# A 31-tap convolution moved from VectorE to 32-column matmuls on TensorE, and a decay's fall computed on ScalarE

## The chip, the core and the metric

The kernel runs on one core of a Trainium2 chip. A core has TensorE (PE: matmuls, results in PSUM; its weight loads are shown apart as PEld), VectorE (DVE), ScalarE (ACT), GpSimd (POOL) and SyncE (SP), each with its own instruction queue worked off in program order, and 16 DMA engines that they share. Engines wait for one another on semaphores. The metric is the device time of the whole program in microseconds.

## The reference

Two blocks follow each other on a sequence of 512 frames with 1024 features: a Mamba-2 layer, a windowed attention layer, then a layer with a convolution and pooling mixer and a feed-forward part, then a layer with an HGRN2 mixer and a feed-forward part. What the change touches:

```
# mamba2_mixer -> ssd_chunked: 32 heads in 8 groups, chunks of 128 frames
a_cs  = cumsum(dt * A) within a chunk                  # falls within the chunk
seg   = a_cs[..., :, None] - a_cs[..., None, :]
decay = exp(where(causal, seg, -inf))
y_diag = einsum((C B^T) * decay, x)
y_off  = einsum(C, h_in, exp(a_cs))

# conv_pool_mixer: z = h @ w_in  (512 value, 512 gate, 512 pool channels)
a = a_val * sigmoid(a_gate)
a = causal depthwise convolution of a, 31 taps, 512 channels, + dw_b
a = silu(layernorm(a, ln_g, ln_b))
for window w in (2, 4, 8, 16), 128 channels each:
    d = mean of the last w frames of u - u;   p = (d @ pool_w[g]) * pool_scale
return concat([a, p]) @ w_out
```

## The kernel before

Features lie on the 128 partitions and the 512 frames on the free axis, so a "tile" is 128 features by 512 frames. All projections are one stream of matmuls with weights from HBM. A float32 weight w is split in two (`wh`, and `wl` = the rest), and so is the activation (`hh`, `hl`); each product is three matmuls (L644 to L646, in the first units of a phase L613 to L615). A unit is 256 columns of a weight. It is loaded in two halves through a ring of four slots: SP loads a half into `stage` (L510), POOL writes `wh` and the negated `wl` (L566, L567) and issues a DMA that adds `stage` onto `wl` (L570). PE makes one tile with 8 x 3 matmuls per 128 columns and puts it in one of four PSUM banks `gp`; DVE takes it out, times `rstd`, and gives the bank back. Nothing plans the order at run time: each engine's program is written out, and generators interleave the projection's granules (half a tile each) with the mixer's own work (`run(gran, n)`).

**Mamba (`mamba`).** The loop goes over 8 groups g and one more round; in each round there are six slots. The projection's tiles of group g are made while the mixer works on group p = g - 1. In slot 0 PE transposes x and B and multiplies C B^T (`turn_and_cb`, L705 to L716); this waits for the SiLU (L1154) of the last of the four short convolutions (L1589, DVE). In slots 1 and 2 PE spreads `a_cs` of two heads each over the partitions (`spread`, L727, banks `mp0` and `mp1`). ACT makes `EC` = exp of it (L1170). DVE picks the chunk's last value (`cd`, L1619) and writes the fall within the chunk to `G`, four pieces of 128 columns a head (`segment`, L1623: min and subtract). ACT takes exp of `G` (L1174), and DVE multiplies (`products`, L1631 and L1633). In slot 2 DVE also carries the states (`recur`, L1637 to L1644). `y_tile` (L748, L752) is in slots 4 and 5: two heads side by side, each with 64 of the 128 output partitions.

**Convolution and pooling (`conv_pool`, called "cp" below).** The projection has 12 tiles: sigmoid gates 0 and 1, values 2 and 3, gates 4 and 5, values 6 and 7, pool channels 8 to 11. The gated values go to `apad` (c_a) with 30 zero columns in front. Channel tiles 0, 1 and 2 are convolved on DVE, one instruction per tap (L1928, L1932: 31 x 3), and the takes of projection tiles 4 to 11 are placed after every fourth tap. Channel tile 3 is convolved on PE (L877): 31 float32 matmuls of 128 x 128 diagonal matrices, which ACT builds before its sigmoids (L1277). POOL computes the window means (`window_means`, L529 to L549) in its queue behind the second unit of the output projection. After the four pool matmuls (L884) and the four matmuls that sum the channels (L891), a layernorm on DVE and ACT, and the output projection.

**Start.** The parameters come in 19 small DMAs, 9 on ACT's queue (behind one for the identity) and 10 on SP's, ahead of the first weights on SP's queue.

Of the kernel before, what the change touches and what calls it, by code (L numbers as in the profile page):

```python
# [34 lines left out]
P = 128  # L35
# [17 lines left out]
CW = 31  # L53
POOLW = (2, 4, 8, 16)
# [13 lines left out]
N_PAR = 19  # L68
# [121 lines left out]
def build(nc, x, positions, pre_norm, post_norm, ssm_w_in, ssm_conv_w, ssm_conv_b, ssm_dt_bias,  # L190
# [50 lines left out]
    with ExitStack() as ctx:  # L241
# [27 lines left out]
        class Region:  # L269
# [74 lines left out]
        apad = R.take("c_a", [P, 4, CW - 1 + L])  # L344
# [7 lines left out]
        taps = R.take("c_taps", [P, CW, P])  # L352
# [62 lines left out]
        taps_ready, gated_ready, last_conv, last_ready, pool_step = (sem(s) for s in (  # L415
            "taps_ready", "gated_ready", "last_conv", "last_ready", "pool_step"))
# [50 lines left out]
        def load_parameters(eng, half):  # L467
# [17 lines left out]
            else:  # L485
                rows(0, 0, P, ssm_conv_w.rearrange("o k (t p) -> (o k t) p", p=P))
                rows(1, 0, CW * 4, cp_dw_w.rearrange("o k (t p) -> (o k t) p", p=P))
# [41 lines left out]
        def window_means(pool):  # L529

            steps = 0
            for g in range(4):
                tile_taken(pool, tiles_of("cp")[0] + 8 + g)
                src, w = ub[:, g, :], 1
                while w < POOLW[g]:
                    dst = ws[:, 0 if w in (1, 4) else 1, :]
                    pool.tensor_tensor(dst[:, 2 * w - 1:], src[:, 2 * w - 1:], src[:, w - 1:16 + L - w],
                                       ALU.add).then_inc(pool_step, 1)
                    steps += 1
                    pool.wait_ge(pool_step, steps)  # L540
                    src, w = dst, 2 * w
                d = window_out(g)
                pool.tensor_scalar(d, src[:, 16:], 1.0 / w, 1.0, ALU.mult, ALU.mult).then_inc(pool_step, 1)
                pool.wait_ge(pool_step, steps + 1)
                pool.tensor_tensor(d[:, 0:16], src[:, 16:32], cst[:, C_RC + 16 * g:C_RC + 16 * g + 16],
                                   ALU.mult).then_inc(pool_step, 1)
                steps += 2
                pool.wait_ge(pool_step, steps)
                pool.tensor_tensor(d, d, ub[:, g, 16:], ALU.subtract).then_inc(window_ready, 1)  # L549

        @block.gpsimd
        def _(pool):
            count = [0] * HALVES
            for q, (u, i) in enumerate(halves):
# [22 lines left out]
                if u == phases["cp_out"][0] + 1:  # L577
                    window_means(pool)
# [3 lines left out]
        def _(pe):  # L582
# [90 lines left out]
            for k in range(KT):  # L673
                if k == 4:
                    pe.wait_ge(par_landed, 16 * N_PAR)
                    pe.wait_ge(skip_ready, 1)
                    for s, rows in enumerate((P, CW * 4, P, 48)):
                        mm = pe.transpose(mp[0][:, s * P:s * P + rows], prow[0:rows, s, :], ident[0:rows, 0:rows])
                    mm.then_inc(prm_turned, 1)
# [191 lines left out]
            def conv_pool():  # L871
                run(h_granules("cp", "pre2", LEAD["cp"], lambda: sum_squares(pre_round[2])))

                pe.wait_ge(gated_ready, 4)
                for i in range(CW):
                    pe.wait_ge(taps_ready, i + 1)
                    mm = pe.matmul(mp[1][:, :], taps[:, i, :], apad[:, 3, i:i + L], start=(i == 0), stop=(i == CW - 1))  # L877
                mm.then_inc(last_conv, 1)
                pe.wait_ge(poolw_landed, 16)
                for g in range(4):  # L880
                    pe.wait_ge(window_ready, g + 1)
                    if g >= 2:
                        pe.wait_ge(hi_ready, split0["cp"] + g - 1)
                    pe.matmul(mp[2 + g % 2][:, :], poolw[:, g, :], window_out(g), start=True,  # L884
                              stop=True).then_inc(pool_ready, 1)
                for t in range(4):
                    if t < 3:
                        pe.wait_ge(conv_ready, t + 1)
                    else:
                        pe.wait_ge(last_ready, 1)  # L890
# [150 lines left out]
        def _(act):  # L1041
# [82 lines left out]
            def mamba():  # L1124
# [46 lines left out]

                def decay_between(g, h):
                    act.wait_ge(seg_ready, 4 * g + h + 1)
                    act.activation(G[:, h, :], G[:, h, :], ACT.Exp).then_inc(dec_ready, 1)  # L1174
# [1025 lines left out]
```

## Time and profile before

| | us |
|---|---|
| median of 3 runs (2032.0 to 2037.17) | 2033.22 |
| the profiled execution, its own time | 2037.46 |
| its span, first to last instruction | 2035.7 |
| PE busy / weight loads | 1889.5 / 1497.6 |
| DVE busy | 1184.6 |
| POOL busy | 937.8 |
| ACT busy | 584.5 |

The span covers nearly all of the execution's own time (1.8 us lie around it). The profiled execution is 4.2 us (0.2%) above the median. PE is busy for 93% of the span, but a busy PE is not always a PE at full rate: the granted clock has a mean of 0.967. Of the slices of 50 us, most between 950 and 1600 us have PE busy from end to end; the mamba phase lies at about 60 to 440 us and the convolution's at about 785 to 950 us.

### The profile page before, as it was taken

The page shows a single profiled execution, that of the slowest core. Times are in us where ns is not written, and L with a number is a line of the kernel's source. Part 1 is how long each engine was busy: PE and PEld are TensorE (multiplying, and loading weights), DVE is VectorE, ACT ScalarE, POOL GpSimd, SP SyncE. Part 2 cuts the span into 40 slices and gives each one's busy share as a digit, 9 for nine tenths or more (in the row PEclk, how much of TensorE's full clock was granted, in tenths as well). Part 3 has the DMA queues.
Part 4 walks back from the last instruction along what each step waited for, and adds up shares of the span by engine and source line. Part 5 has one row for each costly group of instructions (what it writes and reads, how often), then busy time and mean ns, then how long its engine had stood idle before and what let it go on. Part 6 is the DMA issues. An engine that isn't in the chain of part 4 may idle for free.

```text
span 2035.7 us, 24615 instructions
## 1 busy us (share of the span) xinstructions
PE 1889.5 (93%) x9408; PEld 1497.6 (74%) x9408; DVE 1184.6 (58%) x1890; ACT 584.5 (29%) x980; POOL 937.8 (46%) x934
## 2 busy tenths in 40 slices
PE   6999999897899987968999999999999899999997
PEld 5777777686577665725888888887777678888886
DVE  5889898862877756896433231246777763323202
ACT  4333333421433325113201100024666531111001
POOL 4443434344533235552555555654443245555552
PEclk9999999898999998988999999999999899999999
DMA  8767666567445445812888888887555378888884
GB/s 206 163 135 154 134 148 134 124 135 176 109 104 104 94 95 120 194 42 60 199 196 188 197 191 191 196 201 168 125 125 114 88 157 191 196 190 195 184 188 112
DMA packets 207988, 306.31 MB, mean 150 GB/s; under 512 B 20836, under 2 KB 163200, under 8 KB 207872
## 3 DMA queue, kind: packets, MB, share of 16 engines
q0 software_dynamic: 42912, 149.44, 43.0%
q1 hardware_dynamic: 163472, 153.78, 24.0%
q8 instruction: 75, 1.23, 0.2%
q10 hardware_dynamic: 1488, 1.52, 0.2%
q14 instruction: 41, 0.34, 0.1%
HBM read 153.18 MB, written 2.10 MB: 76 GB/s over the span
## 4 chain that ended last, share of the span: by engine, by line
PE 52%; DVE 7%; ACT 2%; issue 1%; POOL 0%; ACTq 0%; DVEq 0%; POOLq 0%
PE gp L644 16%; PE gp L645 15%; PE gp L646 15%; DVE c_acc L1932 4%; PE mp L944 1%; PE gp L614 1%; PE gp L613 1%; PE gp L615 1%; ACT c_taps L1277 0%; PE mp L985 0%; PE mp L994 0%; POOL sqsum L524 0%; ACT L1079 0%; PE mp L987 0%; PE mp L963 0%
## 5 line engine op out<-in xcount | busy, mean ns | idle before, releaser
L566 POOL TENSOR_SCALAR wh<-stage 128x1024 fp32r<-128x1024 f32 (+2 forms) x298 | 352.5, 1183 | 931.6 <-PE gp L646 893.6
L644 PE MATMUL gp<-hh,wh 128*128 128x512 f32 x1544 | 621.2, 402 | 15.4 <-POOL wh L566 5.4
L645 PE MATMUL gp<-hh,wl 128*128 128x512 f32 x1544 | 604.2, 391 | 0.0
L646 PE MATMUL gp<-hl,wh 128*128 128x512 f32 x1480 | 579.4, 392 | 0.0
L644 PEld LDWEIGHTS gp<-hh,wh 128*128 128x128 f32 x1544 | 292.3, 189 | 83.4 <-issue 17.2
L567 POOL TENSOR_SCALAR wl<-stage 128x1024 fp32r<-128x1024 f32 (+2 forms) x298 | 352.5, 1183 | 0.0
L645 PEld LDWEIGHTS gp<-hh,wl 128*128 128x128 f32 x1544 | 292.3, 189 | 59.5 <-issue 1.2
L646 PEld LDWEIGHTS gp<-hl,wh 128*128 128x128 f32 x1480 | 279.4, 189 | 60.1
L570 POOL DMA_DIRECT2D wl<-stage x298 | 264.1, 886 | 94.7 <-POOL wl L567 85.8
L1979 DVE TENSOR_TENSOR val<-gp,rstd 128x512 f32<-128x512 f32 x44 | 30.4, 692 | 203.9 <-PE gp L646 203.9
L1883 DVE TENSOR_TENSOR xT<-gp,xT 128x512 f32<-128x512 f32 x32 | 22.1, 690 | 211.3 <-PE gp L646 211.3
L644 PE MATMUL gp<-f_h,wh 128*128 128x512 f32 x352 | 137.2, 390 | 0.0
L646 PE MATMUL gp<-f_l,wh 128*128 128x512 f32 x352 | 137.0, 389 | 0.0
L645 PE MATMUL gp<-f_h,wl 128*128 128x512 f32 x352 | 136.9, 389 | 0.0
L1056 ACT ACTIVATE f_h<-val 128x512 fp32r<-128x512 f32 x44 | 27.2, 633 | 277.1 <-DVE val L1985 277.1
L1975 DVE TENSOR_TENSOR sq<-gp,rstd 128x512 f32<-128x512 f32 x44 | 30.2, 691 | 114.2 <-PE gp L646 95.0
L1932 DVE SCALAR_TENSOR_TENSOR c_acc<-c_a,prm,c_acc 128x512 f32<-128x512 f32 x90 | 91.0, 1055 | 1.1
L1589 DVE SCALAR_TENSOR_TENSOR m_xs<-m_raw,prm,m_xs 128x512 f32<-128x512 f32 x96 | 84.3, 878 | 2.3
L646 PEld LDWEIGHTS gp<-f_l,wh 128*128 128x128 f32 x352 | 66.1, 188 | 13.7
L644 PEld LDWEIGHTS gp<-f_h,wh 128*128 128x128 f32 x352 | 66.1, 188 | 13.7
L645 PEld LDWEIGHTS gp<-f_h,wl 128*128 128x128 f32 x352 | 66.1, 188 | 13.6
L1985 DVE TENSOR_TENSOR val<-val,sq 128x512 f32<-128x512 f32 x44 | 72.7, 1692 | 0.0
(320 smaller groups left out, 2864.0 us busy)
## 6 DMA issues: line engine op xcount, KB each, us to landing
wl<-stage POOLq DMA_DIRECT2D x264, 512.0 KB, 5.4
stage<-ffn_w SPq DMA_DIRECT2D x120, 512.0 KB, 4.2
stage<-ssm_w_in SPq DMA_DIRECT2D x32, 512.0 KB, 5.1
stage<-hg_w_in SPq DMA_DIRECT2D x32, 512.0 KB, 4.3
stage<-ssm_w_in SPq DMA_DIRECT2D x32, 256.0 KB, 4.1
stage<-ssm_w_out SPq DMA_DIRECT2D x16, 512.0 KB, 4.8
stage<-att_w_in SPq DMA_DIRECT2D x16, 512.0 KB, 4.4
stage<-cp_w_in SPq DMA_DIRECT2D x12, 512.0 KB, 4.9
```

The lines of the kernel that those rows point to most:

```text
L566: pool.tensor_scalar(wh[:, s, part], stage[:, s, part], 1.0, 1.0, ALU.mult, ALU.mult).then_inc(hi_done, 1)
L567: pool.tensor_scalar(wl[:, s, part], stage[:, s, part], -1.0, 1.0, ALU.mult, ALU.mult).then_inc(neg_done, 1)
L570: pool.dma_start(wl[:, s, part], stage[:, s, part], accum_op=ALU.add).then_inc(lo_landed[s], 16)
L644: pe.matmul(bank[:, :], wvh[:, cols], hi(kk), start=start, stop=False)
L645: pe.matmul(bank[:, :], wvl[:, cols], hi(kk), start=False, stop=False)
L646: mm = pe.matmul(bank[:, :], wvh[:, cols], lo(kk), start=False, stop=stop)
L1056: act.activation(dst, val[:, n % 2, :], ACT.Copy).then_inc(hi_ready, 1)
L1589: ins = dve.scalar_tensor_tensor(v, raw[:, n % 2, i:i + L], prm[:, col:col + 1], v, ALU.mult, ALU.add)
L1932: ins = dve.scalar_tensor_tensor(acc[:, c, :], src, w, acc[:, c, :], ALU.mult, ALU.add)
L1975: dve.tensor_tensor(sq[:, j, :], gp[t % 4][:, :], rstd[:, :], ALU.mult).then_inc(bank_read[t % 4], 1)
L1979: dve.tensor_tensor(value_slot(n0 + 2 * n + j), gp[t % 4][:, :], rstd[:, :], ALU.mult).then_inc(bank_read[t % 4], 1)
L1985: dve.tensor_tensor(value, value, sq[:, j, :], ALU.mult).then_inc(value_ready, 1)
```

## The change

1. **Mamba's fall within a chunk goes to ACT.** `segment` on DVE becomes `chunk_decay`, which keeps the `cd` copy alone. ACT computes relu(f - value) from PSUM, four pieces a head, where f is the fall at the row's frame; its sign is turned back by `scale=-1.0` in the exp.

2. **The convolution goes to PE for all four channel tiles.** Four taps and 32 channels are put together on the 128 partitions: `shifted[t]` holds, for block b of 32 channels, four copies of it that are shifted by 0 to 3 frames. 16 DMAs a tile, of 32 partitions x 540 columns each, bring them from `apad`; ACT issues them. One matmul then does 4 taps of 32 channels (a 128 x 32 weight matrix, 512 frames) into 32 of the 128 PSUM partitions; 8 tap groups x 4 blocks are 32 matmuls a tile. DVE builds each tile's weights with one multiplication of 128 x 1024 (`tap_matrix`). ACT adds the bias from PSUM. The first two tiles are convolved between projection tiles, the others behind them.

3. **The window means go from POOL to DVE**, each behind the take of its tile.

4. The tap parameters come in 9 DMAs instead of one (27 parameter DMAs instead of 19), in pieces of 32 numbers, all on SP's queue. `shifted` lies where `ch` and `cl` are written later.

```
+                def fall_within(g, h):
+                    if h == 0 and g == 0:
+                        act.wait_ge(tok_ready, 1)
+                    for c in range(NCH):
+                        s = slice(c * P, (c + 1) * P)
+                        f = tokT[:, 0, c, HPG * g + h:HPG * g + h + 1]
+                        ins = act.activation(G[:, h, s], mp[h % 2][:, s], ACT.Relu, bias=f, scale=-1.0)
+                    ins.then_inc(seg_ready, 1)
...
                         if g > 0 and slot in (1, 2):
                             for h in pair:
                                 decay_to_start(p, h)
+                                fall_within(p, h)
...
-                    for c in range(NCH):
-                        s = slice(c * P, (c + 1) * P)
-                        f = tokT[:, 0, c, HPG * g + h:HPG * g + h + 1]
-                        ins = dve.tensor_scalar(G[:, h, s], mp[h % 2][:, s], f, f, ALU.min, ALU.subtract)
```

On PE:

```
+                def convolve(t):
+                    pe.wait_ge(taps_ready, t + 1)
+                    pe.wait_ge(shifts_landed[t], 16 * SHIFTS * SHIFTS)
+                    if t >= 2:
+                        pe.wait_ge(conv_ready, t - 1)
+                    for m in range(8):
+                        for b in range(SHIFTS):
+                            mm = pe.matmul(mp[t % 2][b * CB:(b + 1) * CB, :], taps[:, m, t, b, :],
+                                           shifted[t % 3][:, b, m * SHIFTS:m * SHIFTS + L],
+                                           start=(m == 0), stop=(m == 7))
+                    mm.then_inc(conv_whole, 1)
+
+                run(gran, 16)
+                convolve(0)
+                run(gran, 4)
+                convolve(1)
+                run(gran)
+                convolve(2)
                 pe.wait_ge(poolw_landed, 16)
                 for g in range(4):
                     pe.wait_ge(window_ready, g + 1)
...
+                convolve(3)
+                pe.wait_ge(conv_ready, 3)
```

On ACT, in place of the 31 diagonal matrices:

```
+                def shift(t):
+                    act.wait_ge(gated_ready, 2 * (t // 2 + 1))
+                    if t == 3:
+                        act.wait_ge(conv_whole, 1)
+                    for d in range(SHIFTS):
+                        for b in range(SHIFTS):
+                            act.dma_start(shifted[t % 3][d * CB:(d + 1) * CB, b, :],
+                                          apad[b * CB:(b + 1) * CB, t, d:d + GW]).then_inc(shifts_landed[t], 16)
...
                 for half in range(2):
                     for j in range(2):
                         t = t0 + 4 * half + j
                         tile_taken(act, t)
                         act.activation(sig[:, j, :], sig[:, j, :], ACT.Sigmoid).then_inc(sig_ready, 1)
+                    shift(2 * half)
+                    if half == 0:
+                        shift(1)
+                add_bias(0)
+                shift(3)
+                add_bias(1)
+                add_bias(2)
```

On DVE:

```
+                def tap_matrix(t):
+                    cols = prm[:, P_DW:P_DW + P].rearrange("p (m r) -> p m r", m=8)[:, :, SHIFTS * t:SHIFTS * (t + 1)]
+                    step(dve.tensor_tensor(taps[:, :, t, :, :],
+                                           eye[:, :].unsqueeze(1).unsqueeze(1).to_broadcast([P, 8, SHIFTS, CB]),
+                                           cols.unsqueeze(3).to_broadcast([P, 8, SHIFTS, CB]), ALU.mult))
...
                 for i in range(4):
                     take(i)
                 gate(0)
-                for n in convolve((0, 1)):
-                    if n % 4 == 2:
-                        take(4 + n // 4)
-                    if n == 15:
-                        gate(1)
-                for n in convolve((2,)):
-                    pass
+                for i in range(4, 8):
+                    take(i)
+                    tap_matrix(i - 4)
+                gate(1)
+                for g in range(4):
+                    take(8 + g)
+                    window(g)
+                dve.wait_ge(conv_whole, 4)
```

How the order of instructions moves. On ACT in slots 1 and 2 of mamba, before (m_EC is `EC`, m_G is `G`, m_tokT holds f):

```order
L1170 ACTIVATE m_EC<-mp 128x512 x2
L1147 ACTIVATE m_xs<-m_raw,prm 128x512
L1174 ACTIVATE m_G<-m_G 128x512 x2
L1170 ACTIVATE m_EC<-mp 128x512 x2
L1147 ACTIVATE m_xs<-m_raw,prm 128x512
L1174 ACTIVATE m_G<-m_G 128x512 x2
L1154 ACT_TABLE_LOAD
```

The same place on ACT in the changed kernel:

```order
L1170 ACTIVATE m_EC<-mp 128x512
L1178 ACTIVATE m_G<-mp,m_tokT 128x128 x4
L1170 ACTIVATE m_EC<-mp 128x512
L1178 ACTIVATE m_G<-mp,m_tokT 128x128 x4
L1147 ACTIVATE m_xs<-m_raw,prm 128x512
L1183 ACTIVATE m_G<-m_G 128x512 x2
L1170 ACTIVATE m_EC<-mp 128x512
L1178 ACTIVATE m_G<-mp,m_tokT 128x128 x4
L1170 ACTIVATE m_EC<-mp 128x512
L1178 ACTIVATE m_G<-mp,m_tokT 128x128 x4
L1147 ACTIVATE m_xs<-m_raw,prm 128x512
L1183 ACTIVATE m_G<-m_G 128x512 x2
```

Sixteen short activations a group are new in ACT's queue, ahead of the short convolution's last tap (m_xs<-m_raw) and of the exp of `G`; no table load is added. On DVE in slot 1, before:

```order
L1543 TENSOR_TENSOR m_raw<-gp,rstd 128x512
L1619 COPY m_cd<-m_EC 128x4
L1623 TENSOR_SCALAR m_G<-mp,m_tokT 128x128 x4
L1619 COPY m_cd<-m_EC 128x4
L1623 TENSOR_SCALAR m_G<-mp,m_tokT 128x128 x4
L1631 TENSOR_TENSOR m_G<-m_G,m_cbm 128x512
L1633 TENSOR_TENSOR m_EC<-m_EC,m_xs 128x512
```

The same place on DVE in the changed kernel:

```order
L1571 TENSOR_TENSOR m_raw<-gp,rstd 128x512
L1647 COPY m_cd<-m_EC 128x4 x2
L1652 TENSOR_TENSOR m_G<-m_G,m_cbm 128x512
L1654 TENSOR_TENSOR m_EC<-m_EC,m_xs 128x512
L1652 TENSOR_TENSOR m_G<-m_G,m_cbm 128x512
L1654 TENSOR_TENSOR m_EC<-m_EC,m_xs 128x512
```

Nothing stands any more between the copies and the products. On PE behind the last tile of the cp projection, before (c_pw the pool weights, c_dp and c_sig the window means):

```order
L646 MATMUL gp<-hl,wh 128x512
L877 MATMUL mp<-c_a,c_taps 128x512 x31
L884 MATMUL mp<-c_dp,c_pw 128x512 x2
L884 MATMUL mp<-c_sig,c_pw 128x512 x2
L891 MATMUL mp<-c_acc,ones 128x512 x4
```

The same place on PE in the changed kernel (c_s_ are the shifted copies):

```order
L633 MATMUL gp<-hl,wh 128x512
L868 MATMUL mp<-c_s_107,c_taps 32x512 x32
L884 MATMUL mp<-c_dp,c_pw 128x512 x2
L884 MATMUL mp<-c_sig,c_pw 128x512 x2
L868 MATMUL mp<-c_s_105,c_taps 32x512 x32
L891 MATMUL mp<-c_acc,ones 128x512 x4
```

Two of the four convolutions stand here; the other two stand ahead, with 48 projection matmuls (two tiles) between them and 48 behind the second.

## Rows read from the trace of the kernel before

**Rows 1.** Windows: start:end and length, busy (count) per engine, PE clock, DMA share, GB/s
```profile
134.17:168.36 34.19, 34.19 (x187) 26.95 (x186) 32.77 (x52) 11.04 (x17) 16.50 (x16) 1.00 0.73 150
178.02:223.54 45.52, 43.54 (x231) 35.08 (x230) 40.45 (x64) 15.60 (x23) 18.68 (x19) 0.96 0.65 139
811.00:857.00 46.00, 41.22 (x177) 32.92 (x176) 37.70 (x42) 12.40 (x35) 29.52 (x27) 0.99 0.91 205
857.00:923.00 66.00, 40.80 (x99) 19.68 (x98) 64.90 (x70) 5.84 (x9) 33.24 (x28) 0.81 0.20 48
```

**Rows 2.** The chain that ended last, cp phase: start us, us, what
```profile
810.62 9.07 ACT c_taps L1277 x31
...
823.08 1.74 DVE c_acc L1928 x2
...
922.80 3.78 PE mp L891 x4
```

**Rows 3.** Timeline of PE, mamba: start us, us, instruction, [idle before <-releaser]
```profile
134.17 0.72 PE L727 MATMUL mp<-m_acs_hl,m_pick 64*128 64x512 f32 x2
...
170.35 1.07 PE L705 MATMUL mp<-cst,m_xs 128*128 128x128 f32 x8 [1.99 <-ACT m_xs L1154]
178.02 0.72 PE L727 MATMUL mp<-m_acs_hl,m_pick 64*128 64x512 f32 x2
...
392.96 1.94 PE L705 MATMUL mp<-cst,m_xs 128*128 128x128 f32 x8 [7.66 <-ACT m_xs L1154]
```

**Rows 4.** Timeline of DVE, mamba, slots 1 and 2 of one round
```profile
135.33 1.74 DVE L1619 COPY m_cd<-m_EC 128x4 f32<-128x4 f32 x1 [0.36 <-ACT m_EC L1170]
...
139.61 0.68 DVE L1631 TENSOR_TENSOR m_G<-m_G,m_cbm 128x512 f32<-128x512 f32 x1
...
146.70 1.37 DVE L1623 TENSOR_SCALAR m_G<-mp,m_tokT 128x128 f32<-128x128 f32 x4
```

**Rows 5.** Timeline of ACT, mamba, slot 1 of the same round
```profile
134.70 1.09 ACT L1170 ACTIVATE m_EC<-mp 128x512 f32<-128x512 f32 x2 [4.12 <-PE mp L727]
```

**Rows 6.** Groups: line, operation xcount | busy us, mean ns | idle before, releaser
```profile
L1623 DVE TENSOR_SCALAR m_G<-mp,m_tokT 128x128 f32<-128x128 f32 x128 | 43.3, 401 | 0.0
L1277 ACT ACTIVATE c_taps<-cst,prm 128x128 f32<-128x128 f32 x31 | 9.2, 388 | 0.0
```

**Rows 7.** Timeline of PE, mamba: float32 at full width, at 64 columns, then a projection
```profile
82.23 1.06 PE L716 MATMUL mp<-m_xs 128*128 128x128 f32 x8
...
108.08 0.33 PE L748 MATMUL mp<-m_G,m_xdt 128*64 128x128 f32 x2
...
108.56 0.39 PE L752 MATMUL mp<-m_EC,m_Hs 128*64 128x128 f32 x4
108.78 0.39 PE L748 MATMUL mp<-m_G,m_xdt 128*64 128x128 f32 x4
...
353.98 0.39 PE L644 MATMUL gp<-hh,wh 128*128 128x512 f32 x1
...
354.66 0.39 PE L644 MATMUL gp<-hh,wh 128*128 128x512 f32 x1
```

**Rows 8.** Timeline of PE, cp phase
```profile
814.37 0.47 PE L644 MATMUL gp<-hh,wh 128*128 128x512 f32 x1 [1.61 <-POOL wh L566]
...
863.52 26.78 PE L877 MATMUL mp<-c_a,c_taps 128*128 128x512 f32 x62
```

**Rows 9.** Timelines of ACT's queue and DVE, start
```profile
1.19 0.45 ACTq L470 DMA_DIRECT2D cst<-shape_const  x1
...
14.99 2.88 DVE L1512 COPY prow<-skip_raw 16x128 f32<-16x128 f32 x1
```

**Rows 10.** DMA queues: packets, MB, share of 16 engines over the span
```profile
q0 software_dynamic: 42912, 149.44, 43.0%
q1 hardware_dynamic: 163472, 153.78, 24.0%
```

**Rows 11.** Timeline of ACT, cp phase
```profile
890.33 0.69 ACT L1285 ACTIVATE c_acc<-mp,prm 128x512 f32<-128x512 f32 x1 [52.29 <-PE mp L877]
```

More of the change, by code:

```diff
@@ L53 @@
 CW = 31
+SHIFTS = 4
+CB = P // SHIFTS
+GW = L + CW + 1 - SHIFTS
 POOLW = (2, 4, 8, 16)
@@ L343, in build @@
         cl = R.take("c_l", [P, KT, L], F32R)
-        apad = R.take("c_a", [P, 4, CW - 1 + L])
+        R.take("c_gap", [P, 2 * SHIFTS * GW - KT * L])
+        shifted = [nc.alloc_sbuf_tensor_at(f"c_s{i}", [P, SHIFTS, GW], F32, offset=a0 + at)
+                   for i, at in enumerate((KT * L * 4, KT * L * 4 + SHIFTS * GW * 4, 0))]
+        apad = R.take("c_a", [P, 4, CW + L])
         acc = R.take("c_acc", [P, 4, L])
@@ L676, in _ @@
                     pe.wait_ge(skip_ready, 1)
-                    for s, rows in enumerate((P, CW * 4, P, 48)):
+                    for s, rows in enumerate((P, P, P, 48)):
                         mm = pe.transpose(mp[0][:, s * P:s * P + rows], prow[0:rows, s, :], ident[0:rows, 0:rows])
@@ L871, in conv_pool @@
             def conv_pool():
[L872 to L878, printed above, removed]
+                gran = h_granules("cp", "pre2", LEAD["cp"], lambda: sum_squares(pre_round[2]))
+                def convolve(t):
[3 more added lines that the diff above has]
+                        pe.wait_ge(conv_ready, t - 1)
+                    for m in range(8):
+                        for b in range(SHIFTS):
[9 more added lines that the diff above has]
+                convolve(2)
                 pe.wait_ge(poolw_landed, 16)
@@ L1274, in conv_pool, with add_bias @@
                 t0 = tiles_of("cp")[0]
-                for i in range(CW):
-                    col = P_DW + 4 * i + 3
-                    act.activation(taps[:, i, :], ident, ACT.Copy, scale=prm[:, col:col + 1]).then_inc(taps_ready, 1)
+                def shift(t):
+                    act.wait_ge(gated_ready, 2 * (t // 2 + 1))
+                    if t == 3:
+                        act.wait_ge(conv_whole, 1)
[3 more added lines that the diff above has]
+                                          apad[b * CB:(b + 1) * CB, t, d:d + GW]).then_inc(shifts_landed[t], 16)
+                def add_bias(t):
+                    act.wait_ge(conv_whole, t + 1)
+                    act.activation(acc[:, t, :], mp[t % 2][:, :], ACT.Identity,
+                                   bias=prm[:, P_DWB + t:P_DWB + t + 1]).then_inc(conv_ready, 1)
                 for half in range(2):
```

107 lines of the change are left out of this document (43 added, 64 removed).

## The prediction

> **What bounds the kernel now.** I read the page's slices first: PE is busy nearly everywhere, so a gain can only be where PE waits or runs at the half clock. Two such stretches meet the change.
>
> In the convolution's phase the chain of waits runs over DVE from 823.08 us, the first tap, until the channel sums on PE at 922.80 [rows 2]. Ahead of it the chain stands on ACT, which builds its 31 diagonal matrices for 9.07 us before it reaches the sigmoids. The windows say the same: from 857 to 923 us DVE is busy for 64.90 of 66 us while PE does 40.80 us of work at a clock of 0.81 and the DMA share is 0.20 [rows 1]. DVE is the bound here.
>
> In mamba the chain has a hole, so I take one round. From 134.17 to 168.36 us PE is busy without a gap [rows 1]; then it waits 1.99 us for the SiLU behind the last short convolution, and the next round's spread starts at 178.02 [rows 3]. So this round is 43.85 us: 34.19 of work, 1.99 idle, 7.67 for transposes and one projection tile. The following round, 178.02 to 223.54, has the same idle time but 45.52 us and a mean clock of 0.96 [rows 1]: a stretch at the half clock after the wait costs 1.67 us more. Of the six full rounds three are of each kind. In the last round PE waits 7.66 us [rows 3]. DVE works nearly without pause from the spread to that SiLU, and is thus just too late: the bound is shared, and what DVE sheds is worth the wait and no more.
>
> **The change, part by part.**
>
> *Mamba.* DVE loses 128 pieces of 401 ns [rows 6]. In slot 1 they stand between 135.33 and the first product at 139.61 [rows 4]. But DVE's next instruction needs ACT's exp, and ACT now does the pieces itself. Its price: a 128 x 128 activation lasts 388 ns, and 31 follow each other in 9.07 us, 0.293 each [rows 2, 6]. From the first exp at 134.70: two exps (1.09 for both [rows 5]) and eight pieces, 1.09 + 8 x 0.293 = 3.43; the short convolution's tap, about 0.65; the exp of `G`, 0.63. That gives 139.4 for the first product against 139.61: slot 1 saves about 0.2 us, since DVE waits instead of working. In slot 2 ACT has its pieces done while DVE is at the short convolution, so DVE saves its two blocks of about 1.35 us, some 2.7 us [rows 4]. The last short convolution ends about 2.9 us earlier. PE needed 1.99 us, so its wait goes and it becomes the bound with 0.9 us to spare. Gain: 3 x 1.99 + 3 x (1.99 + 1.67) = 17 us, and about 3 of the 7.66 in the last round: 20 us. Bounds: if each piece takes the full 388 ns, ACT is 0.8 us later in slot 1, DVE 2.1 us earlier in sum, still just enough. If ACT's order cost DVE all it sheds, the gain is 0. If the last round's wait went wholly, it is 25. I take 20, from the rows of ACT itself.
>
> A rule speaks against this move. The Trainium skill, "ScalarE: Activation LUTs", section "Rules for kernel authors", wants relu on VectorE and not on ScalarE, where it is said to be up to three times slower per element in bf16. Here, with 128 float32 elements out of PSUM, 401 ns on DVE stand against 388 on ACT [rows 6], so the sum stays.
>
> *Convolution, the matmuls.* A float32 matmul of 512 frames takes 26.78 / 31 = 0.86 us in two records [rows 8]. Four tiles have 128 of them. The question is whether the four blocks of 32 columns run side by side. At full width, eight records over 128 frames (four matmuls) take 1.06 us with the tail; at 64 columns four records, one pair of matmuls, are spaced 0.22 us, from 108.56 to 108.78 [rows 7], where four matmuls one by one take about 0.82 (82.23 to the next projection matmul), so two would take 0.41. Pairs do run together. For four at a time no row exists. Bounds for a tile of 32 matmuls: 8 x 0.86 = 6.9 us four at a time, 13.8 two at a time, 27.6 one by one. I take 6.9, since of the ends it is the one that the pairs fit: two records start within 0.01 us (the row of 108.08).
>
> *Convolution, the timetable.* PE starts projection tile 4 at 814.37 [rows 8]. A projection matmul takes 0.68 / 3 = 0.227 us [rows 7], so a tile is 24 x 0.227 = 5.4 us. Tiles 4 to 7 end at 836.1, the first convolution at 843.0, two tiles at 853.9, the second at 860.8, two tiles at 871.7, the third at 878.6. The pool matmuls are 4 x 0.86, plus about 1 us for ACT's bias (0.69 [rows 11]) and its copies between them: 883. The fourth ends at 890 and the channel sums take 3.78 as before [rows 2]: 893.8. Before they end at 922.80 + 3.78 = 926.6. Gain 32.8 us, and what follows is unchanged.
>
> What must hide in it: (a) ACT's 64 DMA issues. A DMA issue on ACT's queue takes 0.45 us [rows 9], 7.2 a tile. Sigmoids without the matrices are done by about 814, so tiles 0 and 1 are issued by 830, tile 2 behind the gate at about 837 by 845, tile 3 behind the first bias by 853. PE wants them at 836, 854, 872 and 883. Queued behind the issues are the sigmoids of gates 4 and 5, on which only tile 2's gate waits. This holds up to about 0.9 us an issue. (b) DVE's means: at most seven instructions of about 0.7 us behind the take of tile 11 at 872, done by 878, ahead of the pool matmuls. They hid on POOL before, so POOL's shedding them is worth nothing. (c) The transfer: 64 x 69 KB = 4.4 MB. At the plain queue's price (7,800 us of engine time for 153.78 MB) this is 14 us on all 16 engines, at the adding queue's (14,000 for 149.44) 26 us [rows 10], while from 811 to 857 the share is already 0.91 [rows 1]. Much of that is weights fetched ahead of PE, and PE now pauses for two convolutions. Bounds 0 and 14; I take 2 us lost, since four half units are ready or under way when the copies start.
>
> *Start.* Eight more DMAs on SP's queue at about 0.45 us are 3.6 us ahead of the first weights. DVE's first instruction that needs the parameters starts at 14.99 [rows 9], and SP's issues were over long before. Bounds 0 and 3.6; I take 1.5.
>
> *Sum.* -20 - 32.8 + 2 + 1.5 = -49.3. Against the profiled execution's own 2037.46 that is 1988; against the median of 2033.22, 4.2 lower, 1984.
>
> **Rivals.**
>
> *B, two at a time.* The Trainium skill, "TensorE: Matmul & The Clock Gate", section "Part 3: Packing small matmuls — row/col tiling", says that matmuls start and end strictly in program order. As a mechanism here: a float32 matmul is two records [rows 8] for the same columns, and if the second must wait for the first and all others behind it, only two neighbours overlap, however many blocks there are. The spacing of 0.22 us in [rows 7] would come out the same. Then a tile takes 13.8 us, 27.6 more in sum: 1984 + 28 = 2012. Against it: the row of 108.08 in [rows 7] is the timeline cut to 0.01 us, and two records have begun in it, where a stagger would have one. Chance 0.19.
>
> *C, one by one, slower than before.* The 32-column blocks don't overlap at all, or four streams of frames at once cannot be fed. Every tile takes 27.6 us: 4 x 20.7 = 83 more, 2067. It turns into a loss from 6.9 + 49.3 / 4 = 19.2 us a tile. For it is only that no row shows 32 columns; against it are the pairs. Chance 0.07.
>
> *D, mamba gains nothing.* ACT's pieces, the tap behind them and the exp arrive later than DVE's did, and PE's 1.99 us stay or grow: 2004. Against it is slot 2, where DVE is busy elsewhere. Chance 0.10.
>
> *E, the copies are late.* Issues cost 1 us or more, or the transfers crowd out the weights: 14 us, 1998. Chance 0.06. That leaves 0.58 for the forecast, whose own range is 1973 to 1994.
>
> The same page's section gives 2.38 for three column tiles. At that efficiency a tile would take some 8.6 us, and the forecast 7 us more, an estimate from that page.
>
> **Numbers.** The range 1972 to 2013 reaches over D, E and B, and leaves out C and the edges. A difference under 0.3% (6 us) can't be told from none. Faster: all but C and a bad joining of B with D and E, 0.91; within it 0.02; slower 0.07.
>
> **What would show it.** In the changed profile: a convolution of 64 records in about 7.1 us (right), 14 (B), 28 (C); the channel sums' end near 894; mamba rounds of 41.9 us, no idle time ahead of the transposes in slot 0 and no half clock there; DVE idle in slot 1 for ACT. PE idle ahead of a convolution for a DMA would be E. The prediction is wrong if the convolutions take over 10 us each, or if the rounds stay over 43.5.

## The result and the profile after

| | before | after |
|---|---|---|
| median, us (lowest to highest, 4 runs each) | 2034.52 (2032.0 to 2037.17) | 1988.79 (1984.1 to 1990.71) |
| ratio | | 0.9772, 95% 0.975 to 0.9794 |
| profiled execution, own time / span | 2037.46 / 2035.7 | 1990.71 / 1988.7 |

The time lies 4.8 us above the forecast of 1984 and inside the prediction's narrower range of 1973 to 1994. Against the profiled execution the forecast was -49.3 us; it came to -46.75. I follow the program from front to back.

**Mamba.** The first fence is PE's timeline in the changed kernel, the second its windows for one round, in the columns of [rows 1].

```profile
128.74 0.72 PE L714 MATMUL mp<-m_acs_hl,m_pick 64*128 64x512 f32 x2
...
162.77 1.04 PE L692 MATMUL mp<-cst,m_xs 128*128 128x128 f32 x8
170.43 0.72 PE L714 MATMUL mp<-m_acs_hl,m_pick 64*128 64x512 f32 x2
...
370.20 1.94 PE L692 MATMUL mp<-cst,m_xs 128*128 128x128 f32 x8 [4.48 <-ACT m_xs L1154]
```

```profile
128.74:170.43 41.69, 41.69 (x230) 33.51 (x230) 35.52 (x48) 19.28 (x39) 18.41 (x19) 1.00 0.71 152
```

The row of the transposes (L692, L705 in the kernel before) has lost its bracket with the wait of 1.99 us [rows 3], and the round is busy from end to end at the full clock: 41.69 us, against 43.85 and 45.52. All six full rounds last 41.7 us. The last round keeps a wait of 4.48 us of the 7.66. From the first spread to the first of the eighth group it is 403.50 - 88.68 = 314.8 us before and 380.86 - 87.04 = 293.8 after: 21.0 us gained.

Where the pieces went, on DVE and on ACT (timelines, the same round):

```profile
129.90 1.81 DVE L1647 COPY m_cd<-m_EC 128x4 f32<-128x4 f32 x2 [0.36 <-ACT m_EC L1170]
133.58 0.69 DVE L1652 TENSOR_TENSOR m_G<-m_G,m_cbm 128x512 f32<-128x512 f32 x1 [1.87 <-ACT m_G L1183]
```

```profile
129.27 0.60 ACT L1170 ACTIVATE m_EC<-mp 128x512 f32<-128x512 f32 x1 [3.50 <-PE mp L714]
129.76 1.13 ACT L1178 ACTIVATE m_G<-mp,m_tokT 128x128 f32<-128x128 f32 x4
...
132.85 1.22 ACT L1183 ACTIVATE m_G<-m_G 128x512 f32<-128x512 f32 x2
```

DVE now idles 1.87 us in slot 1 for ACT, where it wrote the pieces itself in [rows 4]. From ACT's first exp to the first product it takes 4.31 us; it was 4.91 before and 4.7 in the working. Four pieces last 1.13 us, 0.28 each in a row. What PE waits for is the SiLU behind the last short convolution, first before and then after:

```profile
169.58 0.72 ACT L1154 ACTIVATE m_xs<-m_xs,prm 128x512 f32<-128x512 f32 x1 [1.00 <-DVE m_xs L1589]
```

```profile
160.96 0.72 ACT L1154 ACTIVATE m_xs<-m_xs,prm 128x512 f32<-128x512 f32 x1 [2.56 <-DVE m_xs L1617]
```

It ends 36.1 us after the round's first spread before and 32.9 after: 3.2 us earlier, and 1.1 before PE needs it.

**The convolution's phase.** PE's timeline from the sum of squares ahead of the projection to the channel sums, most projection rows left out:

```profile
782.47 1.12 PE L655 MATMUL mp<-sqsum,ones 128*128 128x512 f32 x2 [0.91 <-POOL sqsum L535]
...
789.77 0.47 PE L631 MATMUL gp<-hh,wh 128*128 128x512 f32 x1 [1.37 <-DMA wl<-stage]
...
818.24 9.85 PE L868 MATMUL mp<-c_s,c_taps 128*32 128x512 f32 x64 [5.40 <-DMA c_s<-c_a]
...
839.14 7.07 PE L868 MATMUL mp<-c_s,c_taps 128*32 128x512 f32 x64
...
866.25 2.33 PE L884 MATMUL mp<-c_sig,c_pw 128*128 128x512 f32 x4
868.51 7.07 PE L868 MATMUL mp<-c_s,c_taps 128*32 128x512 f32 x64
875.52 3.70 PE L891 MATMUL mp<-c_acc,ones 128*128 128x512 f32 x8
```

A tile of 64 records lasts 7.07 us: the four column blocks run side by side. I measure the phase from the sum of squares to the end of the channel sums, so that what came earlier stays out: "the stretch" below. Its start before:

```profile
806.83 1.12 PE L668 MATMUL mp<-sqsum,ones 128*128 128x512 f32 x2 [0.39 <-POOL sqsum L524]
```

Before it is 926.58 - 806.83 = 119.75 us, after 879.22 - 782.47 = 96.75: 23.0 gained. Convolution 0 waits 5.40 us for its copies and then lasts 9.85. The windows show both, and ACT's timeline shows its DMA issues (ACTq):

```profile
812.84:818.24 5.40, 0.00 (x0) 0.03 (x1) 1.99 (x3) 0.00 (x0) 3.09 (x4) 0.89 1.09 246
818.24:828.09 9.85, 9.85 (x65) 2.68 (x65) 0.53 (x1) 1.15 (x2) 0.54 (x1) 0.71 1.01 256
828.09:879.22 51.13, 50.98 (x306) 26.78 (x306) 23.34 (x32) 7.68 (x12) 12.03 (x12) 1.00 0.64 139
```

```profile
794.87 31.92 ACTq L1293 DMA_DIRECT2D c_s<-c_a  x32
826.83 1.15 ACT L1305 ACTIVATE c_sig<-c_sig 128x512 f32<-128x512 f32 x2 [36.61 <-issue]
828.89 10.15 ACTq L1293 DMA_DIRECT2D c_s<-c_a  x16
```

An issue takes 1.00 us in the first 32 and 0.63 in the next 16, against the 0.45 assumed. The chain of waits runs over tile 0's last copy, issued at 811.77 and landed 6.34 us later. In convolution 0, behind the wait, PE has a mean clock of 0.71: part of it runs at the half level.

The two gains are 44 us of the 46.75; 1.6 more lie at the start and 1.7 in the phases between the two (experiment 2). At the end of the channel sums the two traces are 47.4 us apart, at the end of the span 47.0.

### The profile page after: what moved, and what is told of

It is laid out like the page before. It is cut to its first block, busy times and chain, and to the rows that moved or that the text cites. A ratio compares the mean times of both kernels' runs of the same rounds, so it can differ in the third digit from the quotient of the medians.

```text
span 1988.7 us, 24972 instructions
## 1 busy us (share of the span) xinstructions
PE 1880.8 (95%) x9602; PEld 1486.1 (75%) x9602; DVE 1079.9 (54%) x1703; ACT 606.8 (31%) x1080; POOL 905.8 (46%) x912
## 3 DMA queue, kind: packets, MB, share of 16 engines
q8 instruction: 77, 1.26, 0.3%
## 4 chain that ended last, share of the span: by engine, by line
PE 56%; DVE 2%; ACT 1%; ACTq 1%; issue 1%; POOL 0%; DMA 0%; DVEq 0%; POOLq 0%
PE gp L631 16%; PE gp L632 16%; PE gp L633 16%; PE mp L868 2%; PE mp L944 1%; ACTq L1293 1%; PE gp L600 1%; PE gp L601 1%; PE gp L602 1%; PE mp L985 0%; PE mp L994 0%; POOL sqsum L535 0%; DMA c_s<-c_a 0%; DVE h_sm L2115 0%; ACT L1079 0%
## 5 line engine op out<-in xcount | busy, mean ns | idle before, releaser
L555 POOL TENSOR_SCALAR wh<-stage 128x1024 fp32r<-128x1024 f32 (+2 forms) x298 | 345.8, 1161 | 925.2 <-PE gp L633 886.8
L631 PE MATMUL gp<-hh,wh 128*128 128x512 f32 x1544 | 620.3, 402 | 13.2 <-DVE m_raw L1571 4.9
L633 PEld LDWEIGHTS gp<-f_l,wh 128*128 128x128 f32 x352 | 66.1, 188 | 13.8
L600 PE MATMUL gp<-hh,wh 128*128 128x512 f32 x128 | 55.6, 434 | 18.0 <-DVE hl L1497 15.6
```

Source lines behind the costliest of these rows:

```text
L555: pool.tensor_scalar(wh[:, s, part], stage[:, s, part], 1.0, 1.0, ALU.mult, ALU.mult).then_inc(hi_done, 1)
L600: pe.matmul(bank[:, :], wvh[:, cols], hi(k), start=(k == 0), stop=False)
L631: pe.matmul(bank[:, :], wvh[:, cols], hi(kk), start=start, stop=False)
L633: mm = pe.matmul(bank[:, :], wvh[:, cols], lo(kk), start=False, stop=stop)
```

## The experiments

**1. Each half alone.** `mamba_alone` is the kernel before with the pieces on ACT; `cp_alone` is the changed kernel with this undone:

```diff
-                                fall_within(p, h)
...
                     step(dve.tensor_copy(cd[:, h, :], EC[:, h, P - 1::P]))
+                    for c in range(NCH):
...
+                        ins = dve.tensor_scalar(G[:, h, s], mp[h % 2][:, s], f, f, ALU.min, ALU.subtract)
```

> Only the decay's fall moves to ACT, the convolution and the start are those of before. Theory (PE's wait behind the last short convolution goes, and the half clock with it): rounds of 41.7 us, no idle time ahead of the transposes, idle in the last round 4.5 instead of 7.66; 21 us less than before over seven rounds, so about 2013. Rival (the even rounds come from the earlier start of the changed kernel, 1.6 us, which moved the half clock out of them): three of the six rounds stay near 43.4, and the gain is 12 to 17 us.

> Only the convolution and the tap loads are changed, mamba is that of before. Theory (the two gains are independent): 23 us in the convolution's phase and 1.6 at the start, about 2009.5; conv 0 again waits about 5.4 us for its copies. First spread in mamba at 87.0, rounds alternating between 43.85 and 45.5. Rival (start's gain is an accident of mamba's work): first spread back at 88.7, and 2011.

Measured: 2013.73 us, ratio 0.9899 (0.9879 to 0.992), and 2009.88, ratio 0.9874 (0.9857 to 0.9891). The shares of 1.01% and 1.26% make 46 us, and the whole change gives 46: they add up. The view of one source line, the spread, with the start of the first and last of its 32 matmuls, one fence each for before, `mamba_alone`, `cp_alone` and after:

```profile
L727 PE MATMUL mp<-m_acs_hl,m_pick x32: 385/441/497, 88.7 to 410.2; 64*128 64x512 f32 x32
```

```profile
L727 PE MATMUL mp<-m_acs_hl,m_pick x32: 385/441/497, 87.9 to 388.4; 64*128 64x512 f32 x32
```

```profile
L714 PE MATMUL mp<-m_acs_hl,m_pick x32: 384/441/497, 88.8 to 410.5; 64*128 64x512 f32 x32
```

```profile
L714 PE MATMUL mp<-m_acs_hl,m_pick x32: 385/446/497, 87.0 to 387.5; 64*128 64x512 f32 x32
```

First to last is 321.5 and 321.7 us with the pieces on DVE, 300.5 and 300.5 with them on ACT. So 21 us belong to the pieces and none to the start, and the rival of `mamba_alone` falls. The stretch is 119.73 us in `mamba_alone`, as before, and 95.52 in `cp_alone`, where convolution 0 waits 4.28 us. One part of `cp_alone`'s expectation failed: its first spread is at 88.8 and not at 87.0, as its rival had it.

**2. The start.** The changed kernel's first spread was 1.6 us earlier, where I had expected 1.5 later. At its start one row differed: the copy of [rows 9], 2.88 us, took 0.22. `late_start` is the kernel before with eight idle loads more:

```diff
-N_PAR = 19
+N_PAR = 27
+                for m in range(8):
+                    rows(3, 64 + 4 * m, 4, cp_dw_b.rearrange("l (t p) -> (l t) p", p=P))
```

> The kernel before with eight more small parameter loads (4 rows each, read by nobody) on SP's queue ahead of the weights, at 0.3 us each; all else as before. Theory (POOL's first weights, 2.4 us later, no longer meet DVE's small copy at 15.0): the copy falls from 2.88 to about 0.3 us, the parameter transposes start near 15.5 instead of 18.02, first spread in mamba at 87.0 to 87.5 instead of 88.7. Rival (the gain at the start is from the changed layout of the taps, not from the delay): the copy stays 2.88 and the first spread comes 1.5 to 2.5 us late, at 90 to 91.

DVE's timeline of it, and PE's:

```profile
15.31 0.22 DVE L1514 COPY prow<-skip_raw 16x128 f32<-16x128 f32 x1
```

```profile
15.68 1.13 PE L680 MATMUL mp<-cst,prow 128*128 128x128 f32 x4 [1.12 <-DVE prow L1514]
...
25.92 0.76 PE L615 MATMUL gp<-hh,wh 128*128 128x512 f32 x1 [3.89 <-DMA wl<-stage]
```

The copy is short and the transposes start 2.3 us earlier, as the theory said; but PE then waits 3.89 us for the later weights, and the first spread is at 88.2. With the late weights it was at 87.0 to 88.8 in all twelve traces, with the early ones at 88.7 and 87.9. The theory held for the copy and failed for the time: the loads cost nothing that these traces can tell. The 1.6 us of the first comparison lie within this scatter. This single run took 2030.77 us, 4.9 less than before; 6 us lie between mamba and the convolution's phase (sum of squares at 800.32, before 806.83), where nothing was changed. Two executions can drift that far apart there.

**3. Who runs beside whom.** `orders` changes only the order of a tile's 32 matmuls:

```diff
+                    order = [[(m, b) for m in both[0] for b in both[1]],
+                             [(m, b) for half in (0, 2) for m in both[0] for b in (half, half + 1)],
+                             [(m, b) for b in both[1] for m in both[0]],
+                             [(m, b) for n in (0, 2, 4, 6) for b in both[1] for m in (n, n + 1)]][t]
```

> The 32 matmuls of each tile stand in another order: tile 0 as before (tap groups outside, blocks inside), tile 1 two blocks at a time, tile 2 one block behind the other, tile 3 two tap groups of one block, then of the next block. Theory (records that write other column blocks run beside each other, and a record waits only for one of its own block): tile 0 and 3 about 7.0 us each, tile 1 13.8, tile 2 27.6. Rival (strict order: nothing passes a waiting record): tile 0 7.0, tile 1 13.8, tile 2 27.6, but tile 3 about 13.8, since the second tap group of each block holds up the next block. Second rival (the speed has nothing to do with the column blocks: 32-column matmuls are simply short): all four tiles 7.0.

Windows of the four tiles (the counts take in a neighbour):

```profile
819.37:829.23 9.86, 9.86 (x65) 2.70 (x65) 0.83 (x2) 1.15 (x2) 0.00 (x0) 0.71 1.03 264
840.26:852.51 12.25, 12.25 (x66) 3.35 (x65) 5.30 (x6) 0.34 (x1) 3.77 (x4) 1.00 0.91 192
863.54:886.13 22.59, 22.59 (x66) 5.97 (x65) 6.97 (x9) 0.00 (x0) 3.87 (x4) 1.00 0.43 94
890.33:897.47 7.14, 7.14 (x66) 2.52 (x65) 0.00 (x0) 1.90 (x4) 0.00 (x0) 1.00 0.00 0
```

Tile 0 is the half clock case again. One block behind the other costs 22.59 us, two at a time 12.25, so the speed does come from the blocks, and the second rival falls. Tile 3 takes 7.14: the strict order, which gave 13.8, falls too. Both slow orders are faster than I worked out. Windows of PE in the tile that goes block by block suggest why (busy, count, clock, DMA share, GB/s):

```profile
863.50:868.68 5.18, 5.18 (x13) 1.00 0.62 117
868.68:870.40 1.72, 1.72 (x9) 1.00 1.10 181
870.40:873.86 3.46, 3.46 (x10) 1.00 0.89 196
873.86:875.60 1.74, 1.74 (x9) 1.00 0.84 287
```

Each count takes in one or two neighbours; without them these are 12 records in 5.18 us, 8 in 1.72, 8 in 3.46 and 8 in 1.74. One record takes 0.43 us; where a block of 16 ends, its last four run beside the next block's first four. Three such joints save 3 x 4 x 0.43 = 5.2 of 27.6 us, one saves 1.7 of 13.8: 22.4 and 12.1, near what was measured. The trace doesn't name the block of a record; that it is these four is read from the counts.

**4. What makes the copies late.** Two versions of the changed kernel. `fewer_issues` has half the issues, each with twice the partitions; `half_bytes` has all issues with half the bytes. Neither computes the convolution: the first leaves out half of the shifts, the second half of the frames. The matmuls are as many and as long.

```diff
-                    for d in range(SHIFTS):
+                    for d in range(2):
...
+                            rows = slice(2 * d * CB, 2 * (d + 1) * CB)
+                            act.dma_start(shifted[t % 3][rows, b, :],
+                                          apad[rows, t, d:d + GW]).then_inc(shifts_landed[t], 16)
```

```diff
-                            act.dma_start(shifted[t % 3][d * CB:(d + 1) * CB, b, :],
-                                          apad[b * CB:(b + 1) * CB, t, d:d + GW]).then_inc(shifts_landed[t], 16)
+                            act.dma_start(shifted[t % 3][d * CB:(d + 1) * CB, b, 0:284],
+                                          apad[b * CB:(b + 1) * CB, t, d:d + 284]).then_inc(shifts_landed[t], 16)
```

> The changed kernel with 8 copies of 64 partitions a tile in place of 16 of 32: the same bytes, half the issues. The rows are not shifted into their right groups, so the convolution sums the wrong frames. Theory (the issue itself costs 1.0 us on ACT's queue, whatever the bytes): issues of tiles 0 and 1 take 16 us instead of 31.9, convolution 0 starts at 813 without idle time, the channel sums end near 871. Rival (the DMA engines, at 0.92 of their time, hold up the issues and the landing): an issue takes 2 us, the 32 us stay, and PE waits 5 us for the copies as before.

> The changed kernel with all 64 copies, of 284 columns in place of 540; the convolution reads 256 frames twice, so its second half is wrong, its matmuls are as many and as long. Theory (issue cost): issues still take 1.0 us each, 31.9 for the first 32, and PE waits some 4 us ahead of convolution 0. Rival (transfers): issues fall to 0.45 to 0.55 us, the wait is gone, sums end near 871.

A single run each: 1987.24 and 1992.24 us. ACT's queue, first of the one and then of the other:

```profile
797.53 23.06 ACTq L1294 DMA_DIRECT2D c_s<-c_a  x16
```

```profile
798.57 29.32 ACTq L1294 DMA_DIRECT2D c_s<-c_a  x32
```

PE's wait fell to 3.71 and 3.54 us, and the stretches are 93.86 and 94.54. `half_bytes` came out near its theory: 0.92 us an issue and most of the wait still there. `fewer_issues` lies between its theory and its rival: half the issues take 28% less, not 50. The chain of waits in the changed kernel and in `fewer_issues` has the rest:

```profile
811.77 6.34 DMA c_s<-c_a
```

```profile
809.50 9.91 DMA c_s<-c_a
```

Counted from the sum of squares, `fewer_issues` issues tile 0's last copy 5.3 us earlier (24.0 against 29.3), but this copy of 64 partitions needs 9.91 us to land where one of 32 needs 6.34. So 3.6 of the 5.3 us are lost again. With half the bytes in 32 partitions the last copy takes 7.37 us to land, no less than the whole one: in this stretch time to landing doesn't go by the bytes.

The issues themselves have two kinds. In the changed kernel and in `half_bytes` most take 0.61 us, and some, two or three in a row, 1.4 to 1.8. In `fewer_issues` the issues of 64 partitions from 830.15 to 832.75 also take 0.62 us, but of the first 16 only three are under 0.71; their mean is 1.44 and the longest takes 2.62. While POOL of the changed kernel waits for PE and issues nothing, from 818.8 to 839.0, only the pair at 819.70 and 821.31 is long, and all 16 of 828.89 to 839.05 are short; the next, at 839.17, starts just behind POOL's issue at 839.03 and takes 1.77. Whether it is POOL's adding DMA that stretches them was not tried. The landing goes with the load too. Issues of the changed kernel in 795 to 813 us, where the view's DMA share is 1.05, and in 828 to 840, where it is 0.64 (KB, median us to landing):

```profile
c_s<-c_a ACTq DMA_DIRECT2D x17, 67.5 KB, 6.3
```

```profile
c_s<-c_a ACTq DMA_DIRECT2D x17, 67.5 KB, 2.5
```

**5. Two queues.** SP issues half of tile 0's copies, ACT the other half:

```diff
+                if q == copies_after:
+                    sp.wait_ge(gated_ready, 2)
+                    for d in range(SHIFTS):
+                        for b in (2, 3):
+                            sp.dma_start(shifted[0][d * CB:(d + 1) * CB, b, :], ...
...
-                        for b in range(SHIFTS):
+                        for b in range(2 if t == 0 else SHIFTS):
```

> The changed kernel, convolutions where they were, but 8 of tile 0's 16 copies (source blocks 2 and 3) are issued by SP behind the third last weight load of this projection. Theory (tile 0's copies are late because one queue issues them, 17.5 us for 16): ACT's 8 and SP's 8 are issued by 804, the last lands by about 811, PE goes from tile 7 at 812.8 straight into convolution 0, no half clock: 7 to 8 us less, 1981. Rival (the DMA engines' load decides, the landing only takes longer): still 3 us or more of idle time ahead of convolution 0, 1987. Second rival (SP's next weight load, 2 to 7 us late, starves PE): idle time ahead of tile 6 or 8 for DMA stage, 1987 or more.

Measured 1984.54 us, ratio 0.9743 (0.9726 to 0.976), 6.9 us below the changed kernel of the same session (1991.45, `after_again` in experiment 6). SP's queue, and PE at convolution 0:

```profile
795.55 8.57 SPq L527 DMA_DIRECT2D c_s<-c_a  x8
```

```profile
815.26 7.07 PE L875 MATMUL mp<-c_s,c_taps 128*32 128x512 f32 x64
```

No bracket, and 7.07 us instead of 9.85: with the issues spread, the copies are there in time, though the DMA engines are about as loaded (a share of 0.89 from 782 to 815, against 0.93). The last of tile 0's copies is issued by 804.4, 21.0 us behind the sum of squares instead of 29.9. So that one queue issues all 16 is what makes them late. The long issues are still there, up to 1.95 us on ACT's queue and 1.75 on SP's, on both at the same time (797.3 to 802.3); but each queue has only 8 to get through. The late weight load of the second rival did no harm that shows: PE has no idle time at tile 6 or 8. The stretch is 89.96, 6.8 less. It would be more but for a wait of 2.34 us for the weights of tile 4 at 791.65, ahead of the split, and a mean clock of 0.57 from 792 to 796 behind it.

**6. Convolution 0 later.**

```diff
-                run(gran, 16)
+                run(gran, 20)
                 convolve(0)
-                run(gran, 4)
-                convolve(1)
                 run(gran)
+                convolve(1)
                 convolve(2)
```

> Convolution 0 stands behind projection tiles 8 and 9, convolution 1 and 2 behind tiles 10 and 11. Theory (convolution 0 was too early for its copies: 5.4 us idle, 2.9 at the half clock behind it): PE has no idle time before any convolution, no half clock from 812 on, channel sums end 8 us earlier, at 871; about 1981. Rival (the transfers, at 0.94 of the DMA engines, crowd out weights whichever way): PE then waits for weights of tile 8 or 10, and the sums end within 2 us of 879; about 1988.

Measured 1981.67 us, ratio 0.9729 (0.9714 to 0.9745), stretch 88.07. It ran again, beside the changed kernel:

> The version with the later convolutions once more: sum of squares to the end of the channel sums 88 us against 96.7 in the changed kernel, total 1981 to 1983. If copies still came late in some executions (the rival), this stretch would be over 90 us again.

> The changed kernel once more, beside the version with the later convolutions on the same chip. Theory (the 8.6 us between the two traces in the convolution's phase are real): 1988 to 1990, 6 to 9 above the later convolutions. Rival (part of it is the scatter of whole executions, of which the start alone showed 1.8 us): under 4 apart.

1981.61 us (1981.26 to 1984.29), ratio 0.9737 (0.9724 to 0.9751), against 1991.45 (1988.02 to 1993.7), ratio 0.9781 (0.9767 to 0.9794): the intervals don't touch, and the stretches are 89.66 and 95.91. The two are 9.8 us apart, a little more than the 6 to 9 expected. PE in `later_again` (the first row is cut off by the view's window: the convolution has 64 records):

```profile
823.67 6.64 PE L868 MATMUL mp<-c_s,c_taps 128*32 128x512 f32 x60
...
841.78 13.94 PE L868 MATMUL mp<-c_s,c_taps 128*32 128x512 f32 x128
855.65 1.98 PE L883 MATMUL mp<-c_dp,c_pw 128*128 128x512 f32 x4
858.98 2.33 PE L883 MATMUL mp<-c_sig,c_pw 128*128 128x512 f32 x4 [1.34 <-ACT c_u L1315]
```

The wait and the half clock are gone; a small one, 1.34 us, is new, for ACT's scaling behind the queue of tile 3's issues. `paired` goes for it:

```diff
                 convolve(1)
-                convolve(2)
                 pe.wait_ge(poolw_landed, 16)
                 for g in range(4):
+                    if g == 2:
+                        convolve(2)
...
                 add_bias(1)
+                value(0)
+                value(1)
                 add_bias(2)
```

> The version with the later convolutions, and in it the pool matmuls of two groups ahead of convolution 2 and two behind it, with ACT's two first scalings taken out of the queue ahead of the third bias. Theory (PE's 1.39 us ahead of the fourth convolution stood behind ACT's queue of issues): they go, sums end 1.2 us earlier, 1980. Rival (ACT's issues of tile 3, over at 856.3, then hold up pool group 2 as well): same time as with the later convolutions, 1981.7 within 0.5.

1985.97 us, ratio 0.9754 (0.973 to 0.9778). The wait ahead of the last convolution fell from 1.39 us (`conv_later`) to 0.33. The stretch is 88.01 as against 88.07, but it begins with a wait for weights that has nothing to do with the edit, first in `conv_later`, then in `paired`:

```profile
791.01 0.47 PE L631 MATMUL gp<-hh,wh 128*128 128x512 f32 x1 [0.53 <-POOL wh L555]
```

```profile
794.33 0.47 PE L631 MATMUL gp<-hh,wh 128*128 128x512 f32 x1 [1.48 <-DMA wl<-stage]
```

From these rows to the end of the channel sums it is 81.7 and 80.6 us, so the rearrangement gives about the 1.2 us that the theory had, in one trace each. The total doesn't show it: of the 4 us by which it is longer, 2.3 lie ahead of the stretch in the profiled executions (sum of squares at 786.93 against 784.65), and the rest is not explained. The lowest time is that of the later convolutions, some 7 to 10 us below the changed kernel.

**7. The means.** The changed kernel with the window means back in POOL's queue:

```diff
+                if u == phases["cp_out"][0] + 1:
+                    window_means(pool)
...
                     take(8 + g)
-                    window(g)
```

> The changed kernel with the window means back on POOL, where they stood before (behind the fourth half of the output projection's weights). Theory (DVE's means are needed, since PE now comes to the pool matmuls 40 us earlier while POOL reaches its means only at 861.5): at the durations of before, 28 us for the four groups, the last mean is ready at about 889; the channel sums end 20 to 24 us later than 879, about 2011. Rival (the prediction's step: the move is worth nothing either way): 1989, sums at 879.

A single run took 2003.8 us, 12.4 above the changed kernel of the same session, with a stretch of 112.65, 15.9 longer than in the first trace. PE's timeline:

```profile
867.76 2.08 PE L909 MATMUL mp<-c_dp,c_pw 128*128 128x512 f32 x2 [3.33 <-POOL c_dp L561]
...
880.40 2.07 PE L909 MATMUL mp<-c_sig,c_pw 128*128 128x512 f32 x2 [4.91 <-POOL c_sig L561]
```

The direction of the theory is right and its size too large: the means took 859.43 to 880.35, 20.9 us and not 28. In the kernel before, PE waited for POOL's last mean too (the row below), but then it waited 14.20 us more for DVE's convolution, ahead of the channel sums of 922.80, which hid it:

```profile
904.14 2.07 PE L884 MATMUL mp<-c_sig,c_pw 128*128 128x512 f32 x2 [10.13 <-POOL c_sig L549]
```

## Why the prediction was right, and where its terms were off

- **Mamba, -20 predicted, -21.0 measured.** The mechanism held: the wait of 1.99 us and the half clock behind it went in all six full rounds (41.7 us, 41.9 predicted), the last round kept 4.5 of 7.66 (4.7 predicted), and the SiLU that PE waits for came 3.2 us earlier (2.9 predicted). That the moved pieces do it is shown by `mamba_alone`. The split between the slots was less good: in the round above slot 1 saved 0.6 us (0.2 predicted), slot 2 only 1.7 (2.7 predicted), since one product there took 3.26 us instead of 0.69, and the remaining 0.9 came later in the round, where the working had nothing. Relu was no dearer on ScalarE here: a piece takes 395 ns on ACT in the changed kernel (median), 401 on DVE before.
- **The matmuls, 6.9 us a tile, measured 7.07.** The pairs in [rows 7] were a sound reading, but they are of 64 columns; that four blocks of 32 would do the same was a choice, and it came true. Rival B, the strict order, falls by the 7.07 and again by tile 3 of `orders`; rival C falls by the 7.07. The bounds for two blocks at a time and for one behind the other were too high: 13.8 and 27.6 us a tile, measured 12.25 and 22.59.
- **The copies.** This step, "what must hide in it", failed in size. Of the timetable's 32.8 us, 23.0 came: 9.8 are missing, where 2 were allowed. 5.40 are the idle time ahead of convolution 0 and 2.8 its half clock; 0.7 are the 0.17 more of each tile; most of the rest is the four projection tiles ahead of it, 23.1 us instead of 21.8. An issue price was taken from the one row of an idle queue at the start, 0.45 us, while the limit of 0.9 that I named myself was passed: tile 0's issues took 17.5 us instead of 7.2. They also began about 4 late, since the gate's two multiplications on DVE took 4.17 us and had no term; the landing took 6.3 and had no term of its own. It is rival E's mechanism at half its price. Two queues or a later convolution take it back, as `split_queues` and `conv_later` show.
- **Start, +1.5 predicted, nothing measured.** The loads are later, but the copy gets shorter, and the wait that remains is for the weights; what each would be worth alone was not separated.
- **"POOL's shedding them is worth nothing."** This reason was wrong, though it cost the sum nothing. The means on DVE are a condition of the gain: left on POOL they cost 15.9 us of the stretch. That DVE is done ahead of the pool matmuls held, with little to spare (its last mean ends at 864.45, the last two pool matmuls begin at 866.25), but "hid on POOL before" said nothing of whether they would hide there now.

The near hit owes something to errors that cancel. Between the profiled executions the forecast is 2.6 us off: 7.8 short in the convolution's phase, but 1.0 more than forecast in mamba, 3.1 at the start (1.5 lost forecast, 1.6 gained) and 1.1 net in phases that nobody changed. The 1.6 and the 1.1 are no larger than the scatter of experiment 2, and so luck.

## What to carry to other kernels

When work is moved so that PE comes to a place earlier, list every input of that place again with its old finishing time; what was hidden by the old delay is not hidden by the new one. Price a run of DMA issues by issues under the load of that stretch, and give the time to landing a term of its own, then place the consumer behind both: here four half tiles later was worth 7 to 10 us. Fewer and larger copies are no sure way out: here each took longer to issue and to land. A matmul that uses a quarter of PE's columns is cheap only if near neighbours in the program write other column blocks; two in a row to the same block still were (7.14 us a tile), eight were not (22.59).

## What the runs showed of the hardware that I had not expected

- The Trainium skill, "TensorE: Matmul & The Clock Gate", section "Part 3: Packing small matmuls — row/col tiling", lets matmuls start and end strictly in program order. The measurement differs: the order with two tap groups of one block in a row takes 7.14 us a tile, where that rule gives 13.8. By the counts of experiment 3, up to four records of one block can wait while those of the next blocks run.
- The same section of the Trainium skill gives 2.38 for three column tiles; that would make some 8.7 us of a tile, an estimate from that page (the prediction rounded it to 8.6). Four blocks took 7.07, against 22.59 with one behind the other, a factor of 3.2, and 3.9 against the 27.6 of records that never overlap (64 x 0.43).
- A DMA issue on ACT's queue takes 0.61 us undisturbed, for 32 or 64 partitions and for 1136 or 2160 bytes a partition. In loaded stretches (share 1.05) there are bursts of 1.4 to 1.8 us with 32 partitions, on ACT's and SP's queue at the same time, and of up to 2.6 with 64, where the mean of 16 is 1.44.
- In the loaded stretch a copy of 32 partitions lands after 6 to 7 us, whether it has 67.5 or 35.5 KB (medians 6.3 and 6.0); one of 64 partitions and 135 KB takes 8.5 (median, `fewer_issues`).
